# First scores of the grouped attention ahead of the last query projection, and an output projection that begins among the last turned units

## The reference, cut to what matters

```python
def gqa_mixer(h_lat, h_ctx, w_qkv, q_norm, k_norm, w_o, rope, need_ctx):
    def project(h, rotate):
        q, k, v = jnp.split(h @ w_qkv, [...], axis=-1)
        q = rms_norm_2(q.reshape(b, n, GQA_HEADS, GQA_HEAD_DIM), q_norm)
        k = rms_norm_2(k.reshape(b, n, GQA_KV_HEADS, GQA_HEAD_DIM), k_norm)
        if rotate:
            q, k = apply_grid_rope(q, rope), apply_grid_rope(k, rope)
...
    y_lat = block_attention(q_lat, k_all, v_all) @ w_o          # 256 queries, 512 keys
    y_ctx = block_attention(q_ctx, k_ctx, v_ctx) @ w_o          # 256 queries, 256 keys
...
def second_block(...):
    for i in range(DEPTH):                                       # i = 0: gqa, i = 1: mla
        y_lat, y_ctx = mixer(h_lat, h_ctx, ...)
        x = layer_norm(alpha * x + g_a * y_lat, ln_g[i, 0], ln_b[i, 0])
        x = layer_norm(alpha * x + g_m * sq_relu_mlp(x * (1.0 + sc_m) + sh_m, w1, w2), ...)
```

## Time and profile before

| | us |
|---|---|
| median of 3 runs | 2374.55 |
| lowest and highest of them | 2367.37, 2376.17 |
| the profiled execution, its own time | 2367.38 |
| its span in the trace | 2365.6 |
| TensorE busy in the span | 2235.9 (95%) |
| VectorE, ScalarE, GpSimd busy | 1239.0, 691.1, 479.0 |

### The profile page before, as it was taken

The page is one execution under the profiler, slowest core; times in us unless marked ns, Lnnn a source line. Parts: engine busy times, 40 slices in busy tenths (PEclk is TensorE's granted clock), DMA queues, the critical chain, the costliest instruction groups (busy, mean ns, idle before and its releaser), DMA issues.

```text
span 2365.6 us, 33139 instructions
## 1 busy us (share of the span) xinstructions
PE 2235.9 (95%) x13928; PEld 1805.5 (76%) x13928; DVE 1239.0 (52%) x1689; ACT 691.1 (29%) x1530; POOL 479.0 (20%) x259
## 2 busy tenths in 40 slices
PE   7999999999999999999999897889999998998998
PEld 7998788799888977887998644447888884555887
DVE  5675436764445744367653226664443443465666
ACT  2224453122012244532220357522112112262211
POOL 2221112243312211122432000101111110102332
PEclk9999999999999999999999898999999999999999
DMA  7634665564365355655646311022223222202551
GB/s 229 215 136 149 215 250 161 189 231 186 125 183 215 108 183 215 245 161 201 226 179 214 110 47 42 1 71 89 84 95 107 73 81 87 88 26 77 197 197 65
DMA packets 210120, 340.13 MB, mean 144 GB/s; under 512 B 46475, under 2 KB 78198, under 8 KB 209846
## 3 DMA queue, kind: packets, MB, share of 16 engines
q1 hardware_dynamic: 208880, 334.50, 40.8%
q0 software_dynamic: 944, 3.47, 0.4%
q10 hardware_dynamic: 150, 0.04, 0.0%
HBM read 335.90 MB, written 2.10 MB: 143 GB/s over the span
## 4 chain that ended last, share of the span: by engine, by line
PE 57%; ACT 4%; DVE 3%; issue 1%; DVEq 0%; ACTq 0%
PE bank L2057 15%; PE bank L268 13%; PE bank L270 12%; PE bank L269 12%; PE bank L635 3%; PE bank L2060 2%; ACT work L2378 1%; DVE ring_low L256 1%; ACT work L2294 1%; ACT work L1093 1%; DVE cos L2572 1%; PE bank L638 0%; ACT L1093 0%; ACT work L2303 0%; PE bank L928 0%
## 5 line engine op out<-in xcount | busy, mean ns | idle before, releaser
L269 PE MATMUL bank<-hT_high,ring_low 128*128 128x256 f32 (+1 forms) x2032 | 604.0, 297 | 0.0
L269 PEld LDWEIGHTS bank<-hT_high,ring_low 128*128 128x128 f32 x2032 | 387.8, 191 | 12.4 <-issue 0.5
L249 POOL CAST ring_high<-ring 128x2048 fp32r<-128x2048 f32 (+2 forms) x108 | 203.7, 1887 | 712.3 <-PE bank L270 649.8
L256 DVE TENSOR_TENSOR ring_low<-ring,ring_high 128x2048 fp32r<-128x2048 f32 (+2 forms) x108 | 239.0, 2215 | 131.8 <-POOL ring_high L249 131.6
L268 PE MATMUL bank<-hT_low,ring_high 128*128 128x256 f32 (+1 forms) x1008 | 293.5, 291 | 15.4 <-DVE ring_low L256 7.9
L270 PE MATMUL bank<-hT_high,ring_high 128*128 128x256 f32 (+1 forms) x1008 | 285.7, 283 | 0.0
L249 POOL CAST half_high<-ring 128x2048 fp32r<-128x2048 f32 x64 | 128.6, 2013 | 675.4 <-PE bank L270 469.9
L268 PE MATMUL bank<-ring_low,hidden_high 128*128 128x512 f32 x640 | 254.0, 397 | 0.0
L1093 ACT ACTIVATE work<-bank 128x512 f32<-128x512 f32 (+10 forms) x268 | 121.3, 476 | 377.7 <-PE bank L270 320.1
L268 PEld LDWEIGHTS bank<-hT_low,ring_high 128*128 128x128 f32 (+1 forms) x1008 | 190.6, 189 | 26.5 <-issue 17.0
L256 DVE TENSOR_TENSOR ring_low<-ring,half_high 128x2048 fp32r<-128x2048 f32 x64 | 152.7, 2391 | 99.7 <-POOL half_high L249 99.2
(11 more groups left out here) (236 smaller groups left out, 4482.0 us busy)
## 6 DMA issues: line engine op xcount, KB each, us to landing
ring<-w_ff SPq DMA_DIRECT2D x32, 2048.0 KB, 8.0
ring<-mlp_w SPq DMA_DIRECT2D x32, 2048.0 KB, 7.9
ring<-w_in SPq DMA_DIRECT2D x30, 2048.0 KB, 8.1
ring<-w_ada SPq DMA_DIRECT2D x24, 2048.0 KB, 7.7
ring<-w_branch SPq DMA_DIRECT2D x24, 512.0 KB, 6.2
ring<-w_in SPq DMA_DIRECT2D x32, 256.0 KB, 4.2
ring<-w_out SPq DMA_DIRECT2D x4, 2048.0 KB, 7.5
ring<-gqa_w_qkv SPq DMA_DIRECT2D x3, 2048.0 KB, 7.7
```

Of the source, the lines that this page charges most:

```text
L249: nc.gpsimd.tensor_copy(self.high(i), self.part(i, False)).then_inc(self.high_made, 1)
L256: nc.vector.tensor_tensor(self.part(i, True), self.part(i, False), self.high(i).bitcast(F32), ALU.subtract)\
L269: nc.tensor.matmul(out, a[1], b[0], start=False, stop=False)
```

## The change

In layer 0, eight averages and seven swaps stay in the projection's loop, which now ends with group 8. The scores of step 0 of the attention are issued next, then the projection `0a9`, the average `0ms8` and the swap of group 7; the average `0ms9` stands behind the scores of step 1, the swap of group 8 behind those of step 2, the swap of group 9 behind the transposes of step 3. ScalarE and VectorE have the same operations moved in the same way. The last two averages use OT banks, and the swap of group 9 stands in the list of the PT pair behind the first two transposed units. The probabilities of two slots now lie in `z`, and the work space of the norms lies in the second half of `g_turn`. In both layers `wo00` uses an SC bank; its first six chunks are computed in the last U steps before `o7` (two each in layer 0, three each in layer 1), and chunks 6 and 7 after it, each behind the read-out of its own pair. No operation is added or taken away.

```diff
-    before = Carver(g_turn.rearrange("p a b c -> p (a b c)"))
+    before = Carver(g_turn.rearrange("p a b c -> p (a b c)"), 2 * 6 * S)
...
-    g_prob = hT.rearrange("p k s -> p (k s)").rearrange("p (a b) -> p a b", a=8)
+    g_prob = [z[:, n] for n in range(2)] + [hT[:, n] for n in range(2, 8)]
...
-            proj += [f"0a{n}" for n in range(NORMED)]
-            score += [f"0ms{n}" for n in range(NORMED)]
-            turned += [f"0rt{n}" for n in range(NORMED)]
+            proj += [f"0a{n}" for n in range(NORMED - 1)]
+            score += [f"0ms{n}" for n in range(NORMED - 2)]
+            outs += [f"0ms{n}" for n in range(NORMED - 2, NORMED)]
+            turned += [f"0rt{n}" for n in range(NORMED - 1)]
...
         score += [f"{i}s{h}_{u}" for h, u in units]
-        proj += [f"{i}s{h + 1}_{u}" for h, u in units]
-        turned += [f"{i}t{h + e}_{u}" for h, u in units for e in range(2)]
-        outs += [f"{i}o{c}" for c in range(PAIRS)] + [f"{i}wo{t}{h}" for t in range(NT[i]) for h in range(2)]
+        score += [f"{i}wo00"]
+        odd = [f"{i}s{h + 1}_{u}" for h, u in units]
+        both = [f"{i}t{h + e}_{u}" for h, u in units for e in range(2)]
+        proj += odd if i == 1 else odd[:1] + [f"0a{NORMED - 1}"] + odd[1:]
+        turned += both if i == 1 else both[:2] + [f"0rt{NORMED - 1}"] + both[2:]
+        outs += [f"{i}o{c}" for c in range(PAIRS)] + [f"{i}wo{t}{h}" for t in range(NT[i]) for h in range(2)][1:]
...
+    def wo_banks(t, h):
+        return SC if t + h == 0 else OT
...
+            for n in range(NORMED - 1):
+                if n >= 2 and n % 4 == 2:
+                    w = W.arrived(pe, f"0q{n // 4}")
+                project(n, w)
+                if n >= 1:
+                    square_mean(n - 1, SC)
                 if n >= 2:
-                    pe.wait_ge(normed, n - 1)
-                    raw = g_k[:, n - 2] if n < 4 else g_qT[:, n - 4]
-                    mm(PT.claim(pe, f"0rt{n - 2}")[:, 0:S], grid_swap, raw[:, 0:S], True, True).then_inc(PT.full, 1)
+                    swap(n - 2)
...
+        def out_part(i, t, h, ps, chunks):
+            yT = buffers(i)[2]
+            w = W.arrived(pe, f"{i}wo{h}")
+            for c in chunks:
+                last = mm(ps[:, :], yT[:, c, t * P:t * P + P], w[:, c, :], c == 0, c == KD - 1)
+            return last
...
             for n in range(PAIRS * U + LAG[i] + 1):
@@ -2202,16 +2224,26 @@
...
+                if i == 0 and n == 0:
+                    project(NORMED - 1, last_q)
+                    square_mean(NORMED - 2, OT)
+                    swap(NORMED - 3)
+                if i == 0 and n == 1:
+                    square_mean(NORMED - 1, OT)
+                if i == 0 and n == 2:
+                    swap(NORMED - 2)
...
+                if i == 0 and n == LAG[i]:
+                    swap(NORMED - 1)
...
+                    if c == PAIRS - 2:
+                        first_out = SC.claim(pe, f"{i}wo00")
+                        OT.taken(pe, f"{i}o{PAIRS - 3}")
+                left = PAIRS * U + LAG[i] - n
+                if 1 <= left <= U:
+                    parts = {2: (0, 3, 6), 3: (0, 2, 4, 6)}[U]
+                    out_part(i, 0, 0, first_out, range(*parts[U - left:U - left + 2]))
+            return first_out
...
-            attention(i)
-
-
-            OT.taken(pe, f"{i}o{PAIRS - 2}", f"{i}o{PAIRS - 1}")
-            w = [W.arrived(pe, f"{i}wo{h}") for h in range(2)]
+            first_out = attention(i, last_q)
+            for c in range(PAIRS - 2, PAIRS):
+                OT.taken(pe, f"{i}o{c}")
+                last = out_part(i, 0, 0, first_out, [c])
+            last.then_inc(SC.full, 1)
...
-                    if t < NT[i]:
-                        ps = OT.claim(pe, f"{i}wo{t}{h}")
-                        for c in range(KD):
-                            last = mm(ps[:, :], yT[:, c, t * P:t * P + P], w[h][:, c, :], c == 0, c == KD - 1)
-                        last.then_inc(OT.full, 1)
+                    if t < NT[i] and t + h > 0:
+                        out_part(i, t, h, OT.claim(pe, f"{i}wo{t}{h}"), range(KD)).then_inc(OT.full, 1)
                     if t >= 1 and h == 0:
                         pe.wait_ge(x_ready, ln_count[i, 0, t - 1])
                         turn_tile([f"{i}hT{t - 1}{half}" for half in range(2)], t - 1)
...
+                if i == 0 and n == 0:
+                    take_q(NORMED - 1)
+                    deviation(NORMED - 2, OT)
+                if i == 0 and n == 1:
+                    deviation(NORMED - 1, OT)
...
+            for n in range(NORMED - 2):
+                scale_q(n)
                 if n >= 1:
-                    raw = g_k[:, n - 1] if n < 3 else g_qT[:, n - 3]
...
+                if i == 0 and n == 1:
+                    rotate_q(NORMED - 3)
+                    scale_q(NORMED - 2)
+                if i == 0 and n == 3:
+                    scale_q(NORMED - 1)
+                if i == 0 and n == 5:
+                    rotate_q(NORMED - 2)
+                if i == 0 and n == 7:
+                    rotate_q(NORMED - 1)
...
-                    residual(t, 0, OT, f"{i}wo{t}0")
+                    residual(t, 0, wo_banks(t, 0), f"{i}wo{t}0")
```

More of the change, by code:

```diff
@@ L1848, in second_block @@
     early, spare = Carver(hT.rearrange("p a b -> p (a b)")), Carver(chip["work"], m.at - 7 * S)
-    m_prob = early.take(6, 512)
+    m_prob = [early.take(512) for _ in range(6)]
     m_turn = [early.take(4, S), z.rearrange("p a b -> p (a b)").rearrange("p (a b) -> p a b", a=4),
@@ L2107, in gqa_project, with project, square_mean, swap @@
                 turn_gate(0, "ga", n)
[L2108 to L2121 removed]
+            for n in range(NORMED - 1):
[4 more added lines that the diff above has]
+                    square_mean(n - 1, SC)
+                if n >= 2:
+                    swap(n - 2)
+            return w
+        def project(n, w):
+            c = n if n < 2 else (n - 2) % 4
+            gemm_T(PROJ.claim(pe, f"0a{n}")[:, :], w, slice(c * P, c * P + P)).then_inc(PROJ.full, 1)
+        def square_mean(n, banks):
+            PROJ.taken(pe, f"0a{n}")
+            mm(banks.claim(pe, f"0ms{n}")[:, :], K("head_mean"), g_sq[:, n % 2], True, True).then_inc(banks.full, 1)
+        def swap(n):
+            pe.wait_ge(normed, n + 1)
+            raw = g_k[:, n] if n < 2 else g_qT[:, n - 2]
+            mm(PT.claim(pe, f"0rt{n}")[:, 0:S], grid_swap, raw[:, 0:S], True, True).then_inc(PT.full, 1)
         def mla_project():
@@ L2323, in gqa_project, with take_q, deviation @@
                 take_gate(0, "ga", n)
-            for n in range(NORMED + 1):
-                if n < NORMED:
-                    ps = PROJ.arrived(act, f"0a{n}")
-                    copy(g_k[:, n] if n < 2 else g_qT[:, n - 2], ps[:, :])
-                    f(g_sq[:, n % 2], ps[:, :], ACT.Square).then_inc(PROJ.free(f"0a{n}"), 1)
-                if n >= 1:
-                    if n >= 3:
-                        act.wait_ge(normed, n - 2)
-                    scale_of(SC, f"0ms{n - 1}", None, g_rs[:, (n - 1) % 2], 1.0)
+            for n in range(NORMED - 1):
+                take_q(n)
+                if n >= 1:
+                    deviation(n - 1, SC)
+        def take_q(n):
+            ps = PROJ.arrived(act, f"0a{n}")
+            copy(g_k[:, n] if n < 2 else g_qT[:, n - 2], ps[:, :])
+            f(g_sq[:, n % 2], ps[:, :], ACT.Square).then_inc(PROJ.free(f"0a{n}"), 1)
+        def deviation(n, banks):
+            if n >= 2:
+                act.wait_ge(normed, n - 1)
+            scale_of(banks, f"0ms{n}", None, g_rs[:, n % 2], 1.0)
         def mla_project():
@@ L2377, in attention @@
                             part = slice(0, 512) if u < 2 else slice(t * S, t * S + S)
-                            last = f(prob[:, slot, part], ps[:, part], ACT.Exp, bias=neg_max[:, slot, t:t + 1],
+                            last = f(prob[slot][:, part], ps[:, part], ACT.Exp, bias=neg_max[:, slot, t:t + 1],
                                      accum_out=total[:, slot, t:t + 1])
                         last.then_inc(SCORE[e].free(name), 1)
+                if i == 0 and n == 0:
[3 more added lines that the diff above has]
+                    deviation(NORMED - 1, OT)
                 if LAG[i] <= n < PAIRS * U + LAG[i]:
@@ L2584, in attention @@
                         part = slice(0, 512) if u < 2 else slice(t * S, t * S + S)
-                        last = vec.tensor_scalar(prob[:, slot, part], prob[:, slot, part], total[:, slot, t:t + 1],
+                        last = vec.tensor_scalar(prob[slot][:, part], prob[slot][:, part], total[:, slot, t:t + 1],
                                                  None, ALU.mult)
                     last.then_inc(prob_ready, 1)
+                if i == 0 and n == 1:
[7 more added lines that the diff above has]
+                    rotate_q(NORMED - 1)
         prev.mod_done(dve)
```

43 lines of the change are left out of this document (17 added, 26 removed).

## The result

| | before | after |
|---|---|---|
| median | 2376.07 (20 runs) | 2380.73 (20 runs) |
| lowest and highest | 2367.37, 2382.32 | 2374.14, 2389.03 |
| span of the profiled execution | 2365.6 | 2386.0 |

The ratio is 1.0028, 95% interval 1.0017 to 1.0039: 6.7 us slower, 4.0 to 9.3 by the interval; the medians differ by 4.7. The forecast was 4.0. That is a real difference, and well within 0.5%. The forecast named 2378.5, counted from 2374.55, the median of 3 runs; the 20 runs put that median at 2376.07, and the measured 2380.73 lies 2.2 above the named value.

The account below looks back on a forecast made before the run. TensorE, busy 95% of the span, was taken as the bound, so gains come only where it idles or waits. 1.4 + 0.1 + 0.8 + 1.7 = +4.0 on the median 2374.55 gave 2378.5; range 2366 to 2385.

Parts of the forecast that it names:

- The start: Start of layer 0's attention: group 9's swap waits for a bank and holds step 4's scores; +1.4 us, bounds from -4.8.
- Layer 0's output projection: Layer 0's tail: `o7` ends 3.52 later, the norm hangs on it, TensorE waits 2.5 ahead of `hT0`; +0.1 us.
- Layer 1's: Layer 1's output projection: `o7` 4.04 later, TensorE waits 2.4 for tile 0's norm ahead of `hT0`; +0.8 us.
- The clock: The two new waits ahead of `hT0`: one fall of the granted clock counted, +1.7 us, bounds 0 and 3.4.
- It does what it says: Rival: start's 4.8 filled, layer 0's norm not late, TensorE keeps 2.4 and 1.6 in the layers; -8.8, chance 0.12.
- Nothing: Rival: the swap at the start isn't held and the clock doesn't fall; -0.4, 2374.2, chance 0.22.
- Slower than noise: Rival: the lower clock stays over the attention's first pairs, +9, with other terms +13, 2387.5; chance 0.16.
- the roots among the exponentials: Start of layer 0's attention: the skill's figure would make two roots an estimated 5.5 longer; the prediction held to the rows.

Follow-up runs that it names:

- roots together: Against the kernel with only the reordered start: the last two roots made together ahead of step 1's exponentials, group 9's scaling, swap and rotation earlier; 2371.09, ratio 0.9999 to before.
- early chunks only: Against the kernel before: only the output projection of both layers begun early as in the change, start of the attention as before; 2377.47, ratio 1.0017.
- changed again: The changed kernel unaltered, timed and profiled once more on the same chip as the version with extra products in the waits; 2380.39, ratio 1.0031 to before.
- three early chunks: Start as before; chunks 0 and 1 ahead of pair 7's first transposes, chunk 2 ahead of `o7`, the rest behind; 2367.95 against 2371.10 before, ratio 0.9991.
- one early chunk: Start as before; only chunk 0 of the output projection ahead of `o7`, instead of six chunks; 2369.12, ratio 0.9982 to before.
- swap later: Reordered start, output projections as before; swap of group 9 behind step 4's transposes instead of step 3's, its rotation later; 2372.95 against 2371.10 before, ratio 1.0015.
- filled waits: Changed kernel plus four unread float32 products of 256 columns ahead of the wait for tile 0's norm, both layers; 2379.62 against 2380.39 for the changed kernel.

## Why the prediction came out as it did

The queue mechanisms it named are the ones found, and the sum is near the measured value; one term, the clock, came out at about twice its size. Point by point:

- **The start, +1.4.** A is 1.39 longer (1.30 to 1.49 in the other four traces with this start). VectorE's maxima came under the projection (1432.21, while `0a9` ran to 1434.73). The scaling of group 9 is 28.87 after the start of `0a8` against 24.23: 4.6 later, forecast 4.8. The swap of group 9 waited for the copy, and swap and scores took 3.20, forecast 3.0. The event itself is 1.20 later. What the working did not name is the wait of 4.45 for the rotation of group 8. And it put the blame on the bank: the swap moved alone, whose gain was given back, and the roots together, whose gain stayed in the trace, point to the late root, without showing it.
- **Layer 0's output projection, +0.1.** B0 is 0.28 longer where no fall disturbs it (early chunks only); the norm's start follows the start of `o7` by 19.97 (1563.34 - 1543.37), before by 20.64 (1543.53 - 1522.89), less the 0.72 that fell away 19.92. `o7` starts 3.66 later behind the first transposes of pair 7 (10.89 in early chunks only, 7.23 before), forecast 3.52. The wait ahead of `hT0` is 2.37, forecast 2.5.
- **Layer 1's, +0.8.** B1 is 1.01 longer, `o7` 4.19 later (forecast 4.04), the wait 2.37, forecast 2.4.
- **The clock, +1.7.** This is the term that was mis-sized. "I count one fall in the two" was wrong: behind a wait of 2.37 or 2.38 the clock fell six times of six (changed, changed again, early chunks only, two layers each), and C0 and C1 are 2.2 and 1.75 longer, together 4.0, a little over the upper bound of 3.4. Of these the 2.2 of layer 0 were not kept in the trace (582.05 against 581.61, above); from `hT0` of layer 1 to the end of the span it is 210.64 against 208.78, but a kernel without any wait there can be 1.5 over before as well (three early chunks, 2368.4 - 2158.07 = 210.33). Besides, there is a fall that no term had, at the first transposes of pair 7: B0 has 1.56 or 1.57 more with it (33.29 against 31.73, and 33.02 against 31.45). The working had dismissed this place: "the gaps of up to 0.9 in the tail, 3.6 in sum". The sum is that of the window, and it holds one gap of 1.68, larger than 0.9:

```profile
1515.66 1.12 PE L2060 MATMUL bank<-consts,work 128*128 128x128 f32 x8 [1.68 <-ACT work L2294]
```

Behind it the clock fell in all five traces that have the start as changed, and in none of the five others in which TensorE idles as long there (1.68 or 1.69; before, early chunks only, one early chunk, roots together, swap later). Why it goes with the start's order stays open. The same gap was overlooked as room for chunks; the version with three early chunks fills it.

From `0a8` to the end the trace has +6.5, the time 4.7 by the medians and 6.7 by the ratio, against a forecast of 4.0. Of the 6.5, the order makes 2.7 (1.39, 0.28 and 1.01, forecast 2.3), the fall at the transposes 1.6, and what is left, 2.3, lies behind `hT0` in the two layers, 0.4 in layer 0 and 1.9 in layer 1. So the clock is at 3.9 instead of 1.7, and the forecast was low by the clock, not by the queues. That 4.7 lies so near to 4.0 is in part luck, as the interval of the ratio alone is 5.3 wide. How the 2.3 divide between the two waits and the falls that every kernel has is not to be had from single traces.

The rivals: *It does what it says* (-8.8) fell, since `o7` releases the casts, as the prediction had against it; a gain exists, but only for chunks that don't push `o7`. *Nothing* (-0.4) fell by both its conditions: the swap was held, and the clock fell. *Slower than noise* (+13) fell too: the granted clock of the 40 us of the start is 0.79 before and after, and 1.00 in the steady pairs.

On the roots among the exponentials, ScalarE's read of a sum ended at 1443.18 and the load of the next table began at 1443.20 and took 1.28; the whole root was 3.93 long, against 3.96. The Trainium skill, "ScalarE: Activation LUTs", What ACT_TABLE_LOAD costs, has a drain of 1.38 beside the load: no gap of that size stands in these rows. So the loads cost no more here than before; what the order of the roots cost is in who waits for them.

## What to carry to other kernels

Before pulling work of one engine ahead of an instruction, ask what that instruction releases on the others: early chunks were free as long as they fitted TensorE's idle time, and lost where they pushed `o7`, from which a chain of 20 us on GpSimd and VectorE hangs. Moving only the consumer of a late result (the swap) gained nothing here; with its producer moved too (the roots), the trace gained. Compare two traces from an event ahead of the change: here two profiles of one and the same kernel were 9.4 us apart before the first touched instruction. And price a fall of the clock by a stretch that reaches far behind it: of the 2.1 us that C0 gained by filled waits, 0.3 were left 580 us later.

## What the runs showed of the hardware

- Idle times of 2.37 to 2.38 us of TensorE ahead of `hT0` were followed by a fall of the granted clock to the lower level in 6 cases of 6; 0.65 in the same place in 0 of 2, 0.17 and 0.18 in 0 of 2. The fall was expected in one of two.
- An idle time of 2.48 to 2.49 in another place was followed by a fall in 5 traces of 12, and one of 1.68 or 1.69 in 5 of 10. Length alone does not decide.
- Work that only keeps TensorE busy held the clock behind the wait, but a fall came at a later idle time instead (0.66 there, 1.00 in the changed kernel), and the kernel's time did not change by more than the runs can tell.
